# Seven experts' rows scaled by their slots' gates and added to a DRAM buffer by GpSimd's accumulating indirect DMA, in place of TensorE's combine

## The reference

```
logits = t @ w_router; top_v, top_i = top_k(logits, 2); wts = softmax(top_v)
gate = sum(one_hot(top_i, 8) * wts[..., None], axis=1)        # [256 tokens, 8 experts]
for e in range(8):
    ye = (silu(t @ w_gate[e]) * (t @ w_up[e])) @ w_down[e]    # w_gate, w_up [1024, 3584], w_down [3584, 1024]
    out = out + gate[:, e:e + 1] * ye
```

## Time and profile before

| | |
|---|---|
| median of 3 runs | 1756.88 us (1756.1 to 1757.53) |
| profiled execution, its own time | 1759.97 us |
| its span, first to last instruction | 1758.2 us |
| mean granted TensorE clock | 0.995 |
| PE busy | 1738.1 us, 99% |
| DVE, ACT, POOL busy | 1437.6, 1191.4, 119.6 us |
| bytes read from HBM | 474.71 MB |

### The profile page before, as it was taken

How to read it: one execution, slowest core, us unless ns; L and a number is a source line. 1 busy time by engine, 2 the same in 40 slices (tenths; PEclk the granted TensorE clock), 3 DMA queues, 4 the chain that set the end, 5 groups by cost and what they waited for, 6 DMA issues and landing times.

```text
span 1758.2 us, 23343 instructions
## 1 busy us (share of the span) xinstructions
PE 1738.1 (99%) x8758; PEld 1439.0 (82%) x8758; DVE 1437.6 (82%) x1348; ACT 1191.4 (68%) x1405; POOL 119.6 (7%) x165
## 2 busy tenths in 40 slices
PE   9999999999999999999999999999999999999998
PEld 7778888888888888888888888888888888888886
DVE  8997557776649955768898898898998988988987
ACT  7877564744457756567777777767777767777775
POOL 5160000150002200000000000000000000000000
PEclk9999999999999999989999999999999999999999
DMA  7454336655444443479999999999999999999994
GB/s 242 141 167 142 123 122 214 209 185 180 167 162 152 154 151 120 159 265 369 377 351 338 381 362 367 375 343 360 364 354 374 357 350 379 349 373 374 364 370 166
DMA packets 221226, 477.09 MB, mean 271 GB/s; under 512 B 9357, under 2 KB 34057, under 8 KB 221129
## 3 DMA queue, kind: packets, MB, share of 16 engines
q1 hardware_dynamic: 220328, 474.07, 75.3%
q0 software_dynamic: 704, 1.70, 0.5%
q10 hardware_dynamic: 96, 0.02, 0.0%
HBM read 474.71 MB, written 1.05 MB: 271 GB/s over the span
## 4 chain that ended last, share of the span: by engine, by line
PE 88%; DVE 9%; issue 1%; ACT 1%; DMA 0%; SPq 0%; DVEq 0%; ACTq 0%
PE ps L736 27%; PE ps L738 26%; PE ps L737 26%; DVE ring_lo L2048 3%; PE ps L1271 1%; PE ps L1013 1%; PE ps L729 1%; DVE turned L2306 1%; PE ps L985 1%; DVE z L2264 1%; PE ps L1249 1%; PE ps L996 1%; ACT hi_m L1430 0%; DVE lo L2486 0%; PE ps L1345 0%
## 5 line engine op out<-in xcount | busy, mean ns | idle before, releaser
L2486 DVE TENSOR_TENSOR lo<-ring_e,hi 128x2048 fp32r<-128x2048 f32 x288 | 657.6, 2290 | 78.8 <-ACT hi L1788 76.9
L1788 ACT ACTIVATE hi<-ring_e 128x2048 fp32r<-128x2048 f32 x288 | 551.9, 1917 | 164.5 <-PE ps L738 164.5
L736 PE MATMUL ps<-hi,xe_hi 128*128 128x512 f32 x896 | 354.5, 396 | 1.7 <-DVE lo L2486 0.9
L738 PE MATMUL ps<-hi,xe_lo 128*128 128x512 f32 x896 | 349.6, 390 | 0.0
L737 PE MATMUL ps<-lo,xe_hi 128*128 128x512 f32 x896 | 349.0, 390 | 0.0
L1430 ACT ACTIVATE hi_m<-ring 128x1024 fp32r<-128x1024 f32 x160 | 160.6, 1054 | 115.9 <-PE ps L738 112.5
L2048 DVE TENSOR_TENSOR ring_lo<-ring,hi_m 128x1024 fp32r<-128x1024 f32 x160 | 190.2, 1231 | 33.6 <-ACT hi_m L1430 33.1
L738 PE MATMUL ps<-hi_m,xT_lo 128*128 128x512 f32 (+1 forms) x528 | 203.2, 385 | 0.0
L736 PEld LDWEIGHTS ps<-hi,xe_hi 128*128 128x128 f32 x896 | 168.3, 188 | 38.1 <-issue 3.7
L738 PEld LDWEIGHTS ps<-hi,xe_lo 128*128 128x128 f32 x896 | 168.2, 188 | 36.0
L737 PEld LDWEIGHTS ps<-lo,xe_hi 128*128 128x128 f32 x896 | 168.4, 188 | 33.2
(11 more groups left out here) (422 smaller groups left out, 2464.5 us busy)
## 6 DMA issues: line engine op xcount, KB each, us to landing
ring_e<-in_moe_w_gate SPq DMA_DIRECT2D x104, 1024.0 KB, 6.9
ring_e<-in_moe_w_up SPq DMA_DIRECT2D x96, 1024.0 KB, 7.0
ring_e<-in_moe_w_down SPq DMA_DIRECT2D x88, 1024.0 KB, 6.7
ring<-in_w_in SPq DMA_DIRECT2D x50, 1024.0 KB, 5.0
hT<-in_moe_w_down SPq DMA_DIRECT2D x24, 1024.0 KB, 6.1
hT<-in_moe_w_up SPq DMA_DIRECT2D x16, 1024.0 KB, 6.4
ring<-in_ffn_w_gate SPq DMA_DIRECT2D x22, 512.0 KB, 3.9
ring<-in_ffn_w_up SPq DMA_DIRECT2D x22, 512.0 KB, 4.8
```

Source lines behind the costliest of these rows:

```text
L736: nc.tensor.matmul(o, x_hi, w_hi, start=first, stop=False, skip_group_check=True)
L738: return nc.tensor.matmul(o, x_lo, w_hi, start=False, stop=end, skip_group_check=True)
L1788: nc.scalar.activation(hi[:, m % H, :], src, ACT.Copy).then_inc(sem("hi_ready"), 1)
L2486: last = V.tensor_tensor(lo[:, m % H, :], src, hi[:, m % H, :].bitcast(F32), ALU.subtract)
```

## The change

For experts 0 to 6 the transposes, `dispT`, `y_lo`, the eight combine matmuls and `add_rows` go. Instead:

- Once, POOL builds token numbers and ones in `routes` and copies x to the DRAM buffer `sums` (256 rows, and 128 spare rows) by two DMAs. DVE puts the gate's high and low part beside them in `route_weights` (two more instructions).
- In each expert PE multiplies `disp` by the four columns of `routes`: two matmuls of 4 columns, which give each slot's token number, its occupancy, and its gate in two parts. DVE copies these 128 x 4 values (`slot_values`), and POOL makes from them the row number (a spare row if the slot is empty) and the gate, with five small instructions.
- ACT copies y from PSUM to `y_rows`, scaled by the slot's gate. POOL issues one indirect DMA that adds the 128 rows of 4 KB to `sums`.
- After seven of them POOL loads `sums` back into x. The last expert combines on TensorE as before.

```
+                for e in range(NE - 1):
+                    pool.wait_ge(sem("slot_values_taken"), e + 1)
+                    chain(nc.gpsimd.tensor_scalar(row_of[:], slot_values[:, 1:2], -1.0, 1.0, ALU.mult, ALU.add))
+                    chain(nc.gpsimd.tensor_tensor(row_of[:], row_of[:], spare_row[:], ALU.mult))
+                    chain(nc.gpsimd.tensor_tensor(row_of[:], row_of[:], slot_values[:, 0:1], ALU.add))
+                    if e > 0:
+                        pool.wait_ge(sem("rows_added"), 16 * e)
+                    chain(nc.gpsimd.tensor_copy(row_i[:], row_of[:]))
+                    nc.gpsimd.tensor_tensor(slot_gate[:], slot_values[:, 2:3], slot_values[:, 3:4], ALU.add).then_inc(
+                        sem("slots_ready"), 1)
+                    if e == 0:
+                        pool.wait_ge(sem("sums_set"), 16 * 2)
+                    pool.wait_ge(sem("rows_ready"), e + 1)
+                    pool.indirect_dma_start(sums, bass.IndirectOffsetOnAxis(row_i[:, 0:1], 0), y_rows[:], None,
+                                            compute_op=ALU.add).then_inc(sem("rows_added"), 16)
+                pool.wait_ge(sem("rows_added"), 16 * (NE - 1))
+                pool.dma_start(x[:], sums[0:SEQ].rearrange("(c p) d -> p c d", p=P)).then_inc(sem("x_summed"), 16)
...
 PE, expert():
-                    pe.wait_ge(sem("added"), 4 * e + 1)
-                    for c in range(C):
-                        last = nc.tensor.transpose(ps[:, 3, c * P:(c + 1) * P], disp_plain[:, c, odd, :], ident[:])
+                    if scattered:
+                        pe.wait_ge(sem("added"), 1)
+                        pe.wait_ge(sem("routes_ready"), 1)
+                        pe.wait_ge(sem("route_rows_ready"), 1)
+                        if e > 0:
+                            pe.wait_ge(sem("slot_values_taken"), e)
+                        for c in range(C):
+                            last = nc.tensor.matmul(ps[:, 3, 0:4], disp[:, c, odd, :], routes[:, c, e, :], start=c == 0,
+                                                    stop=c == C - 1)
+                        last.then_inc(sem("slot_values_done"), 1)
...
                     if not last_one:
                         gate_first(e + 1)
+                    if scattered:
+                        pe.wait_ge(sem("rows_ready"), e + 1)
+                        return
...
 ACT, expert():
+                    if scattered:
+                        act.wait_ge(sem("slots_ready"), e + 1)
+                        if e > 0:
+                            act.wait_ge(sem("rows_added"), 16 * e)
+                        act.wait_ge(sem("split_used"), M + s0 + MOE_TILES)
+                        nc.scalar.activation(y_rows[:], flat_banks(4, 2), ACT.Copy, scale=slot_gate[:]).then_inc(
+                            sem("rows_ready"), 1)
...
 DVE, route_weights() and expert():
+                chain(V.tensor_copy(routes[:, :, :, 2], gate[:]))
+                V.tensor_tensor(routes[:, :, :, 3], gate[:], routes[:, :, :, 2].bitcast(F32), ALU.subtract).then_inc(
+                    sem("routes_ready"), 1)
...
-                    if not first_one:
+                    if not first_one and not first_pass:
                         add_rows(e_here - 1, e - 1)
...
+                    if scattered:
+                        dve.wait_ge(sem("slot_values_done"), e + 1)
+                        if not first_one:
+                            dve.wait_ge(sem("slots_ready"), e)
+                        V.tensor_copy(slot_values[:], ps[:, 3, 0:4]).then_inc(sem("slot_values_taken"), 1)
...
                     if last_one:
+                        if first_pass:
+                            dve.wait_ge(sem("x_summed"), 16)
                         add_rows(e_here, e, ADD_BY_HALVES)
```

More of the change, by code:

```diff
@@ L225, in decoder_trunk @@
         slot_ramp = fb("slot_ramp", [P, P])
-        fb("idle", [P, KD - 3, P])
+        routes = fb("routes", [P, C, NE, 4], F32R)
+        token_i = fb("token_i", [P, C], I32)
+        token = fb("token", [P, C])
+        spare_row = fb("spare_row", [P, 1])
+        slot_values = fb("slot_values", [P, 4])
+        row_of = fb("row_of", [P, 1])
+        row_i = fb("row_i", [P, 1], I32)
+        slot_gate = fb("slot_gate", [P, 1])
+        fb("idle", [P, (KD - 3) * P - 128])
         xe_hi = fb("xe_hi", [P, KD, P], F32R)
         xe_lo = fb("xe_lo", [P, KD, P], F32R)
+        y_rows = renamed("y_rows", [P, D], F32)
         y_hi = fb("y_hi", [P, D], F32R)
@@ L245, in decoder_trunk, with combines_before @@
         TURNS = MOE_TILES // RM
+        sums = nc.dram_tensor("sums", [SEQ + P, D], F32).ap()
+        def combines_before(e):
+            return e - (NE - 1)
         def expert_tile(p):
@@ L545, in _ @@
                 o = slice(half * BANK, (half + 1) * BANK)
-                sp.wait_ge(sem("added"), 4 * (NE - 1) + 3 + 2 * half)
+                sp.wait_ge(sem("added"), 3 + 2 * half)
                 sp.dma_start(rows_out[:, :, o], x[:, :, o]).then_inc(sem("stored"), 16)
@@ L712, in _, with expert_rows @@
                     rotary_gains(1)
+            def expert_rows():
+                pool.wait_ge(sem("h_ready"), C)
+                pool.wait_ge(sem("h_hi_ready"), C)
+                chain(nc.gpsimd.iota(token_i[:], pattern=[[P, C]], base=0, channel_multiplier=1))
+                chain(nc.gpsimd.tensor_copy(token[:], token_i[:]))
+                nc.gpsimd.tensor_scalar(spare_row[:], token[:, 0:1], float(SEQ), None, ALU.add)
+                nc.gpsimd.tensor_copy(routes[:, :, :, 0], spread(token[:], 2, NE))
+                nc.gpsimd.tensor_copy(routes[:, :, :, 1], ones[:, 0:C * NE].rearrange("p (c e) -> p c e", c=C)).then_inc(
+                    sem("route_rows_ready"), 1)
+                pool.dma_start(sums[0:SEQ].rearrange("(c p) d -> p c d", p=P), x[:]).then_inc(sem("sums_set"), 16)
+                pool.dma_start(sums[SEQ:SEQ + P], x[:, 0, :]).then_inc(sem("sums_set"), 16)
+                for e in range(NE - 1):
[15 more added lines that the diff above has]
+                pool.dma_start(x[:], sums[0:SEQ].rearrange("(c p) d -> p c d", p=P)).then_inc(sem("x_summed"), 16)
+            expert_rows()
         @block.tensor
@@ L1296, in gate_first, with expert @@
                     hidden(0, FFN_TILES, MOE_TILES * e, e)
-                def expert(pair, odd, last_one):
+                def expert(pair, odd, last_one, scattered=False):
                     e = 2 * pair + odd
@@ L1306, in expert @@
                     hidden(1, M + 2, s0)
-                    pe.wait_ge(sem("added"), 4 * e + 1)
-                    for c in range(C):
-                        last = nc.tensor.transpose(ps[:, 3, c * P:(c + 1) * P], disp_plain[:, c, odd, :], ident[:])
-                    last.then_inc(sem("dispatchT_done"), 1)
+                    if scattered:
[8 more added lines that the diff above has]
+                        last.then_inc(sem("slot_values_done"), 1)
+                    else:
+                        ci = combines_before(e)
+                        pe.wait_ge(sem("added"), 4 * ci + 1)
+                        pe.wait_ge(sem("slot_values_taken"), NE - 1)
+                        for c in range(C):
+                            last = nc.tensor.transpose(ps[:, 3, c * P:(c + 1) * P], disp_plain[:, c, odd, :], ident[:])
+                        last.then_inc(sem("dispatchT_done"), 1)
                     def step(f, shift, first, between=None, gathers=None):
@@ L1334, in expert @@
                         gate_first(e + 1)
-                    pe.wait_ge(sem("dispatchT_ready"), e + 1)
+                    if scattered:
+                        pe.wait_ge(sem("rows_ready"), e + 1)
+                        return
+                    pe.wait_ge(sem("dispatchT_ready"), ci + 1)
                     for c, half in ADD_BY_HALVES if last_one else ADD_BY_ROWS:
@@ L1339, in expert @@
                         elif c == 0 and half == (1 if last_one else 0):
-                            pe.wait_ge(sem("y_ready"), e + 1)
+                            pe.wait_ge(sem("y_ready"), ci + 1)
                         t = slice(c * P, (c + 1) * P)
@@ L1373, in one_pass @@
                         for p in range(NE // 2 - 1):
-                            expert(p, 0, False)
-                            expert(p, 1, False)
+                            expert(p, 0, False, True)
+                            expert(p, 1, False, True)
                     else:
@@ L1379, in one_pass @@
                             expert(p + pair0, 1, False)
-                    expert(NE // 2 - 1 + pair0, 0, False)
+                    expert(NE // 2 - 1 + pair0, 0, False, pair0 == 0)
                     expert(NE // 2 - 1 + pair0, 1, True)
@@ L1386, in experts @@
                 with pe.If(busiest > P):
-                    pe.wait_ge(sem("added"), 4 * NE + 1)
+                    pe.wait_ge(sem("added"), 4 * combines_before(NE) + 1)
                     one_pass(NE // 2)
@@ L1973, in expert @@
```

(51 more changed lines are left out.)

## The result

The changed kernel takes 1759.26 us (median of 22 runs, 1758.1 to 1762.4) against 1756.71 us of the kernel before (22 runs too): the ratio is 1.0014, 95% interval 1.0008 to 1.0020. So it is 2.5 us slower, where 12.3 us less were forecast, and the time lies outside the predicted range.

A forecast was written before the change was run, and what follows sets the result against it. PE (TensorE) was taken to bound the experts' part. Combine -12.7, slot matmuls against transposes 0, route_weights +0.4 and boundary 0 gave -12.3 us, from 1756.88 to 1744.6 us; range 1742.5 to 1752.

The forecast's parts named there:

- the sum: Whole kernel: combine -12.7, slot matmuls against transposes 0, route_weights +0.4, boundary 0, together -12.3 us.
- The combine: End of seven experts: eight matmuls of 1.82 us in all leave PE's path, 12.7 us less.
- The slot matmuls against the transposes: PE, each expert: two 4-column matmuls, 0.21 us, cancel the transposes' 0.22 us; bounds -1.5 to +1.4 us over seven experts.
- The two instructions in route_weights: DVE before expert 0's first low part: 0.4 us more on the path, once; bounds 0 and 0.5.
- The boundary: From one expert to the next: low parts of tiles 2 to 4 ready before PE asks, 0 us; if not, 3.5 in all.
- The scatter: Seven accumulating DMAs of 512 KB after y_rows: taken as 0 us lost; one lasts from 3.7 to 31 us.
- The cover of 7.6 us for a tile: Weight stream: a loaded tile lies ready about 7.6 us before ACT reads it, so shorter delays cost nothing.
- the room which slices of 400 GB/s leave: Weight stream: at 400 GB/s and more a tile can pass in about 2.6 us, making good a delay within the expert.
- The boundary didn't limp: Rival, chance 0.07: ACT or DVE late by 1 us at each of seven changes of expert, 1752 us.
- the scatter didn't stop the stream: Rival, chance 0.10: after each y_rows, DMA engines finish each 4 KB row before weight packets; at 2 us a row, 1803 us.
- the DMA rival: Rival, chance 0.07: DMA at a 374 GB/s ceiling becomes the bound, 1749.5 us; with a ceiling 1% lower, 1757.
- its sign, ACT waiting for landings: Trace sign of DMA as the bound: PE waiting for low parts and ACT's high parts for DMA, spread over the expert.

The follow-up runs named there:

- the aligned kernel: The changed kernel with 32 bytes more in the idle tile, so xe_hi, xe_lo, y_rows and disp stand where they stood before the change: 1744.91 us, ratio 0.9931.
- the runs with one and with four: The changed kernel with its tiles back in place and one accumulating DMA per expert, 1744.91 us, or three more into other DRAM buffers, 1752.26 us.

## Why the prediction was wrong

**The step that failed** is the sum: "-12.7 + 0 + 0.4 + 0". It has no term for where the operands lie, and takes it that every matmul which stays keeps its distance of 0.227 us. In fact the distance rose to 0.233 us in the 2688 matmuls with xe_hi and xe_lo. The missing term is the 32 bytes: +15.0 us in the kernel before (1772.26 against 1757.25) and about +14.4 in the changed one (1759.26 against 1744.91, from two sets of runs). The list of changes doesn't mention the place of the new tiles, and no rival had a cost that is spread over work which isn't edited.

**The other terms held.** With the tiles back in place the kernel takes 1744.91 us, against 1744.6 forecast. The single runs of it spread more than that (1744.19 to 1745.63), so how near the number came is partly luck; the terms are not:

- The combine, -12.7 us: an expert takes 120.2 us against 122.0, and PE waits for nothing but its issue until the last combine.
- The slot matmuls against the transposes, 0 forecast: 0.23 us against 0.22.
- The two instructions in route_weights, +0.4: PE's wait for low parts in expert 0 rose from 0.94 us to 1.27, so by 0.33, a little less:

```profile
784.72 0.50 PE L782 MATMUL ps<-hi,xe_hi 128*128 128x512 f32 x1 [1.27 <-DVE lo L2558]
```

- The boundary, 0: its thin covers of 0.4 to 0.8 us held. DVE's low parts after y_rows in the aligned kernel are back to back or wait for ACT, and PE never waits for them:

```profile
897.79 4.49 DVE L2558 TENSOR_TENSOR lo<-ring_e,hi 128x2048 fp32r<-128x2048 f32 x2 [0.89 <-ACT hi L1850]
903.01 4.64 DVE L2558 TENSOR_TENSOR lo<-ring_e,hi 128x2048 fp32r<-128x2048 f32 x2 [0.73 <-ACT hi L1850]
```

- The scatter, 0 between bounds of 3.7 and 31 us: it lands in 11 us and costs nothing. The cover of 7.6 us for a tile is borne out by the runs with one and with four; that the reason is the room which slices of 400 GB/s leave was argued and not tested.

**The rivals.** The boundary didn't limp; the DMA wasn't the bound (the aligned kernel is 12 us faster with the same stream); the scatter didn't stop the stream. The measured time resembled the DMA rival's (nearly all the gain gone), for another reason: its sign, ACT waiting for landings, is missing.

**PE's two reads.** The Trainium skill ("SBUF — State Buffer", Who interferes with whom) gives PE two independent read ports, one for the moving operand and one for the weights, and says that PE never waits on anyone. The trace agrees as far as other engines go: in the kernel before the matmuls start 0.227 us apart beside busy ACT and DVE (902.22 to 902.90) and just as much behind their last tiles (1746.73 to 1748.77). That the two reads are independent of each other it doesn't bear out: they cost about 5.6 ns a matmul, 15 us in 1757, when the operands stood 32 bytes off, and the price was there with PE alone at work.

## What to carry to other kernels

When PE is the bound, a small tile declared in front of others is an edit of every matmul: work out where the stationary and the moving operands stand before and after, and keep their distance a multiple of 256 bytes, which cost nothing here (float32r, blocks of 128 x 128 against 512 columns; other types and widths weren't tried). Padding tiles that look idle may be doing just that. And if removed work doesn't come back as time while no wait has grown, compare the duration and the spacing of the instructions that were not touched.

## What the runs showed of the hardware

- 2688 f32r matmuls of 512 columns at full clock (1.00 in the earlier trace rows): 0.227 us apart with the two operands a multiple of 256 bytes apart; with the stationary one 32, 64 and 128 bytes lower they cost 15.0, 4.8 and 13.5 us in all, about 5.6, 1.8 and 5.0 ns each. Why the price isn't in the order of the offsets was not settled; where in the memory the two reads meet was not shown either.
- An accumulating indirect DMA of 128 rows of 4 KB lands after 9.6 to 11.5 us beside the weight stream (364 GB/s from 903 to 1021 us of the changed kernel). Its issue keeps POOL busy for 1.7 to 2.2 us.
- POOL's instructions on one column take 0.19 us, or about 2.1 to 2.3 us when DVE is just then making a low part from two tiles of 2048 columns, as in these rows of the changed kernel. It was hidden here, for POOL had 100 us.

```profile
793.35 0.19 POOL L744 TENSOR_TENSOR row_of<-row_of,slot_values 128x1 f32<-128x1 f32 x1
...
911.87 2.32 POOL L744 TENSOR_TENSOR row_of<-row_of,slot_values 128x1 f32<-128x1 f32 x1
```

```profile
911.85 2.28 DVE L2558 TENSOR_TENSOR lo<-hT,hi 128x2048 fp32r<-128x2048 f32 x1
```
